# A two-layer decoder trunk: the stretch behind the experts, with tail products tile by tile, rows scaled by ScalarE, the last stores on two queues, the first gathers counted apart, and the final vector loaded in the rotary tables' place

## The reference

```python
for layer in range(2):
    # even: conv mixer + forgetting attention; odd: sparse attention, rotary on q/k and the indexer's q/k
    hp = hp + mixer(rms_norm(hp, norm_mix))          # odd: proj = h @ w_in_odd, 4*512 + 72 columns
    x2 = rms_norm(hp, norm_ffn[layer])
    # 16 experts; top group, then the top 2 experts in it; combine (m, 16) has two weights a row
    y = sum(combine[:, e:e+1] * ((silu(x2 @ w_gate[e]) * (x2 @ w_up[e])) @ w_down[e]) for e in range(16))
    hp = hp + y
y_prompt = rms_norm(hp, norm_final)                  # y * rsqrt(mean(y*y) + 1e-6) * gain
```

## Time and profile before

| | us |
|---|---|
| median of three timed runs | 1640.16 |
| lowest and highest of them | 1635.81, 1641.26 |
| the profiled execution, its own time | 1629.98 |
| span of the profile | 1628.2 |
| mean granted TensorE clock, share of full | 0.915 |

### The profile page before, as it was taken

How to read it: one execution, slowest core, us unless ns; L and a number is a source line. 1 busy time by engine, 2 the same in 40 slices (tenths; PEclk the granted TensorE clock), 3 DMA queues, 4 the chain that set the end, 5 groups by cost and what they waited for, 6 DMA issues and landing times.

```text
span 1628.2 us, 28717 instructions
## 1 busy us (share of the span) xinstructions
PE 1389.5 (85%) x11123; PEld 787.1 (48%) x11124; DVE 645.3 (40%) x1541; ACT 300.5 (18%) x773; POOL 145.7 (9%) x370
## 2 busy tenths in 40 slices
PE   7999668888958999989589987888999699998990
PEld 4444434444445554655254443455545455555650
DVE  2059944332143311111265899566412432111104
ACT  2110024332010000000111211445521000000002
POOL 0059100000000000000200000000000000000002
PEclk9999678999978999999889999799999699999995
DMA  8440127778154899999811021233332487999965
GB/s 268 173 169 1 58 67 230 226 231 297 47 201 161 326 368 368 399 398 416 309 38 52 1 100 61 76 105 105 105 155 98 141 309 286 396 386 390 404 272 197
DMA packets 86635, 341.60 MB, mean 210 GB/s; under 512 B 24791, under 2 KB 32055, under 8 KB 72534
## 3 DMA queue, kind: packets, MB, share of 16 engines
q1 hardware_dynamic: 66302, 289.80, 48.4%
q0 software_dynamic: 10656, 37.56, 6.8%
q10 hardware_dynamic: 9536, 12.33, 2.2%
HBM read 309.53 MB, written 30.47 MB: 209 GB/s over the span
## 4 chain that ended last, share of the span: by engine, by line
PE 55%; DVE 20%; DMA 10%; SPq 7%; issue 5%; ACT 2%; POOL 1%; ACTq 0%; DVEq 0%; POOLq 0%
PE banks L1098 18%; PE banks L1126 9%; PE banks L1027 7%; DVE arena L2148 6%; DMA arena<-in_wstream 6%; PE banks L796 4%; DVE arena L1665 4%; SPq L446 3%; PE banks L827 3%; DVE arena L1793 2%; SPq L472 2%; PE banks L946 2%; DMA arena<-hn_scratch,arena 2%; DVE arena L1787 1%; SPq L477 1%
## 5 line engine op out<-in xcount | busy, mean ns | idle before, releaser
L1098 PE MATMUL banks<-arena 128*32 128x128 f32 (+1 forms) x4736 | 363.3, 337 | 28.1 <-issue 17.3
L1098 PEld LDWEIGHTS banks<-arena 128*32 128x32 f32 (+1 forms) x4736 | 241.5, 127 | 148.4 <-issue 59.2
L1126 PE MATMUL banks<-arena 128*64 128x512 f32 (+1 forms) x1184 | 175.8, 503 | 1.1 <-ACT arena L1551 1.1
L1665 DVE TENSOR_TENSOR arena<-arena,banks 128x256 f32<-128x256 f32 (+5 forms) x84 | 38.9, 464 | 295.4 <-PE banks L1098 171.0
L796 PE MATMUL banks<-arena 128*128 128x512 f32 x320 | 139.9, 595 | 1.0 <-DMA arena<-in_wstream 0.9
L2042 DVE COPY arena<-banks 128x256 f32<-128x256 f32 (+1 forms) x56 | 21.4, 382 | 289.7 <-PE banks L1111 283.3
L1665 DVE TENSOR_TENSOR arena<-banks,arena 128x512 f32<-128x512 f32 (+5 forms) x159 | 70.6, 474 | 141.1 <-ACT arena L1475 86.6
L1665 DVE TENSOR_TENSOR arena<-arena 128x256 f32<-128x256 f32 (+17 forms) x248 | 98.7, 431 | 57.6 <-ACT arena L1416 36.1
L827 PE MATMUL banks<-arena 128*128 128x512 f32 x256 | 118.1, 607 | 0.0
L1027 PE MATMUL banks<-arena 128*128 128x512 f32 x256 | 111.2, 594 | 1.4 <-issue 0.8
L2148 DVE SCALAR_TENSOR_TENSOR arena<-arena 128x512 f32<-128x512 f32 x120 | 105.2, 937 | 1.1
(11 more groups left out here) (269 smaller groups left out, 1493.8 us busy)
## 6 DMA issues: line engine op xcount, KB each, us to landing
arena<-in_wstream SPq DMA_DIRECT2D x109, 2048.0 KB, 16.0
arena<-in_fox_kt SPq DMA_DIRECT2D x64, 256.0 KB, 2.9
arena<-in_fox_v SPq DMA_DIRECT2D x64, 256.0 KB, 3.0
arena<-in_dsa_page SPq DMA_DIRECT2D x64, 256.0 KB, 2.9
expert_rows<-arena ACTq DMA_DIRECT2D x76, 128.0 KB, 8.9
expert_rows<-arena POOLq DMA_DIRECT2D x1, 6656.0 KB, 20.2
hn_scratch<-arena POOLq DMA_DIRECT2D x8, 512.0 KB, 3.0
expert_rows<-arena ACTq DMA_DIRECT2D x72, 32.0 KB, 8.5
```

The lines of the kernel that those rows point to most:

```text
L1098: last = mm(bank(b, 0, 4 * n, n * j, n * j + n), x[:, c, :], w[:, c, 4 * n * j:4 * n * j + 4 * n], start=(c == 0), stop=(c == DC - 1))
L1126: last = mm(bank(3, 0, 8 * n, n * q, n * q + n), ht2[g % 2][:, 128 * i + n * j:128 * i + n * j + n], w[:, c, 8 * n * q:8 * n * q + 8 * n], ...
L1665: return v.tensor_tensor(out, x, y, op)
```

## The change

- Layer 0: TensorE's transposes and tail products alternate. It turns tile 0, then for each tile t turns tile t+1 and computes the tail products of tile t. The tail weights are waited for at the first product.
- Layer 0: the scaling of rows moves from VectorE to ScalarE (`scaled`, a copy with the inverse root as scale). VectorE only inverts the root and signals `inverse`; its loop has `NT + 2` steps and does `to_xt` for tile t-2, ahead of the reciprocal of tile t-1, for which it waits in the same step.
- SP loads tail weights and constants of layer 1 when the row numbers are known (`row_u0`) instead of when all tiles are combined. In its queue they stand behind `last_rows(0)`.
- Both layers: of the four pieces of the last part ScalarE stores two and SP the other two (`last_rows`).
- Both layers: the first gather has a semaphore of its own, `yb_first`, and VectorE waits for the first two gathers one by one.
- The final vector goes to the region of the rotary tables, the causal mask and the router weights instead of `XT`, and is issued when the normalised rows of layer 1 are stored, behind the last expert weights. It, and both tail weights, share the semaphore `c_late`.

```diff
 PER = {stem: n for n, stems in SHARED for stem in stems.split()}
-PER_PARITY = {"hn_out": (48, 32), "yb": (32,) * NT,
+PER_PARITY = {"hn_out": (48, 32), "yb": (16,) + (32,) * (NT - 1),
               "y_rows": tuple(max(STORED[i::4]) for i in range(4))}
...
     nlf = at("WORK", 4160, 64, 0, 8)
-    fin_g = at("XT", 0, 1024)
+    fin_g = at("ROPE", 0, 1024)
     yfin = [at("X", 2048 + 1024 * i, 1024) for i in range(NT)]
...
             tokens(t)
-        sp.dma_start(at("WORK", 3072, 64), a["wtail0"]).then_inc(S("c_tail0"), 16)
+        sp.dma_start(at("WORK", 3072, 64), a["wtail0"]).then_inc(S("c_late"), 16)
         sp.dma_start(bvec, a["bvec"]).then_inc(S("c_misc"), 16)
...
+        def last_rows(l):
+            s, off, n = PARTS[GROUPS - 1]
+            i, r0 = (GROUPS - 1) % 4, 32 * FIRST[s] + off
+            sp.wait_ge(S(f"y_ev{l}"), upto(f"y_ev{l}", GROUPS))
+            for q in range(64 // n, 128 // n):
+                sp.dma_start(y_d[r0:r0 + n, 8 * n * q:8 * n * q + 8 * n], y2[i][n * q:n * q + n, 0:8 * n])\
+                    .then_inc(S(f"y_rows{l}_{i}"), 16)
         def spilled(l):
...
             sp.dma_start(ring[k % RING], a["wstream"][k]).then_inc(S(f"ring{k % RING}"), 16)
+        last_rows(0)
         spilled(0)
-        sp.wait_ge(S("combined0"), NT)
-        sp.dma_start(at("WORK", 3072, 576), a["wtail1"]).then_inc(S("c_tail1"), 16)
+        sp.wait_ge(S("row_u0"), 1)
+        sp.dma_start(at("WORK", 3072, 576), a["wtail1"]).then_inc(S("c_late"), 16)
...
         experts(1)
+        sp.wait_ge(S("hn_out1_0"), upto("hn_out1_0", 48))
+        sp.dma_start(fin_g, a["fin_gain"]).then_inc(S("c_late"), 16)
+        last_rows(1)
         spilled(1)
-        sp.wait_ge(S("combined1"), upto("combined1", 1))
-        sp.dma_start(fin_g, a["fin_gain"]).then_inc(S("c_fin"), 16)
         for t, c0, c1 in TILES:
...
                                             bass.IndirectOffsetOnAxis(row_u[0:rows(t), NT * k + t:NT * k + t + 1], 0))\
-                        .then_inc(S(f"yb{l}_{t}"), 16)
+                        .then_inc(S(f"yb{l}_{t}") if i else S("yb_first"), 16)
...
                     after(job)
-            pe.wait_ge(S("c_tail0"), 16)
+            pe.wait_ge(S("c_late"), 16)
             for t, c0, c1 in TILES:
...
-            pe.wait_ge(S("c_tail1"), 16)
+            turn_h(2, 0)
             for t, c0, c1 in TILES:
+                if t + 1 < NT:
+                    turn_h(2, t + 1)
+                if t == 0:
+                    pe.wait_ge(S("c_late"), 32)
                 pe.wait_ge(S("xt2"), upto("xt2", t + 1))
...
         spilled(0)
-        for t in range(NT):
-            turn_h(2, t)
...
+            def scaled(t):
+                act.wait_ge(S("inverse"), t + 1)
+                if t - 1 > 0:
+                    act.wait_ge(S("hn_t2"), upto("hn_t2", t - 1))
+                af(hn[t % 2][0:rows(t), :], h[0:rows(t), t, :], ACT.Copy, scale=rstd[0:rows(t), t:t + 1])\
+                    .then_inc(S("hn2"), 1)
             if n == 0:
...
                         root(t - 1)
+                    if t and n == 2:
+                        scaled(t - 1)
                 else:
...
                 root(NT - 1)
+            if n == 2:
+                scaled(NT - 1)
...
                 act.wait_ge(S(f"y_ev{l}"), upto(f"y_ev{l}", g + 1))
-                for q in range(128 // n):
+                for q in range(128 // n if g < GROUPS - 1 else 64 // n):
                     act.dma_start(y_d[r0:r0 + n, 8 * n * q:8 * n * q + 8 * n], y2[i][n * q:n * q + n, 0:8 * n])\
...
             hv = h[0:rows(t), t, :]
-            dve.wait_ge(S(f"yb{l}_{t}"), upto(f"yb{l}_{t}", 32))
+            if t > 0:
+                dve.wait_ge(S(f"yb{l}_{t}"), upto(f"yb{l}_{t}", 32))
             for k in range(2):
                 i = 2 * t + k
+                if i == 0:
+                    dve.wait_ge(S("yb_first"), 16 * l + 16)
+                if i == 1:
+                    dve.wait_ge(S(f"yb{l}_0"), upto(f"yb{l}_0", 16))
                 ins = v.scalar_tensor_tensor(out=hv, in0=ybuf[i][0:rows(t), :],
...
             n = 2 * l + 2
-            for t in range(NT + 3):
+            for t in range(NT + 2):
                 if t < NT:
...
                     mean_square(n, t - 1)
-                if 2 <= t <= NT + 1 and l == 0:
-                    normed(n, t - 2)
-                if t >= 3 and l == 0:
-                    to_xt(n, t - 3)
-                if 2 <= t <= NT + 1 and l == 1:
+                if t >= 2 and l == 0:
+                    to_xt(n, t - 2)
+                if 1 <= t <= NT and l == 0:
+                    dve.wait_ge(S("root2"), upto("root2", t))
+                    cell = rstd[0:rows(t - 1), t - 1:t]
+                    v.reciprocal(cell, cell).then_inc(S("inverse"), 1)
+                if 2 <= t and l == 1:
                     final(t - 2)
...
             if t == 0:
-                dve.wait_ge(S("c_fin"), 16)
+                dve.wait_ge(S("c_late"), 48)
             v.scalar_tensor_tensor(out=yfin[t][0:rows(t), :], in0=h[0:rows(t), t, :],
```

## The result

Over 17 runs each, the kernel after has a median of 1624.83 us (1617.27 to 1629.39), the kernel before 1632.00 (1623.87 to 1646.82). The ratio is 0.9935, 95% interval [0.9913, 0.9957]: 0.65% faster, where the forecast was 0.35%. It rested on the first three runs of the kernel before, whose median of 1640.16 lies 8.2 us above that of the 17. So the time misses mainly by its starting point, and the ratio is the better measure of the change.

What follows compares the result with a forecast made beforehand. TensorE, busy 85% of the 1628.2 us span, was taken as the bound. Gains of 3.9 (layer 0) and 1.9 (layer 1) sum to 5.8 us, off a 1640.16 median: 1634.4, range 1629.5 to 1641.

Steps and rivals of the forecast that it cites:

- I take the gain as the same number of microseconds: 1634.4: Whole kernel: the 5.8 us gain is taken off the three-run median of 1640.16 us, giving 1634.4.
- so I put the rise at 823.1: Layer 0's combine: TensorE's clock returns to full at 823.1 us, 4.4 us after dense work starts.
- layer 0's 3.9: Layer 0's tail products, tile by tile: end at 834.8 against 838.7 us, 3.9 earlier; bounds 1 and 4.7.
- rival C: Layer 0: clock rises late or queue order costs more; gains 1.5 there, 1.9 in layer 1, 1636.8 us; chance 0.20.
- Rival B: Layer 0: clock stays at half, products end 4.9 us later than before; whole 1643.2 us; chance 0.08.
- Rows scaled by ScalarE: Layer 0's loop: 4.5 us a tile against 4.6, copy 1.06 us; VectorE wins nearly nothing.
- Stores: Both layers' last stores, split over two queues: 0.9 us earlier each, within 0.7 to 1.0.
- rival D: Stores gain nothing, from SP's block load or slower landing; gain 4.2 in all, 1636.0 us; chance 0.12.
- First gather apart: Both layers: VectorE's first operation comes early, but the 1.3 us is hidden by tile 1's wait; worth 0.
- constants: Layer 1's constants and tail weights, loaded before layer 0's gathers: costed at 0, or 1 us without cover.
- Final vector: Layer 1's end: early issue removes VectorE's wait, tile 3 then waits for gathers; gain 1.9 us, bounds 1.7 and 2.4.

Runs made afterwards that it cites:

- fin_late: Changed kernel with the final vector issued late, when tile 0 of layer 1 is combined: ratio 0.9934 to the kernel before.
- stores_one: Changed kernel with all four last stores on ScalarE again in both layers: ratio 0.9964 to the kernel before.
- joint_first: Changed kernel with one semaphore for both first gathers again: pieces 799.8, 44.1, 750.8, 35.0 us.
- es_late: Changed kernel with layer 1's constants loaded when all tiles are combined, tail weights still early: ratio 0.9937 to the kernel before.
- warm: Changed kernel with 24 extra matmuls, results unused, around layer 0's transposes (20, 3 and 1): ratio 0.9946 to the kernel before.
- scale_dve: Changed kernel with VectorE scaling layer 0's rows in its old loop, TensorE's new order kept: ratio 0.9952 to the kernel before.
- alternate_alone: Kernel before with only TensorE's transposes and products alternating and the tail weights loaded early: ratio 0.9963 to the kernel before.
- best3: Changed kernel with VectorE scaling rows in its old loop and layer 1's constants loaded late: ratio 0.9930 to the kernel before.
- before_again: Kernel before, no edit, profiled a second time: layer 0's piece 51.1 us.
- l0_old: Changed kernel with layer 0's loop as before (VectorE scales, all transposes, then all products): ratio 0.9949 to the kernel before.
- products_last: Changed kernel, ScalarE still scaling, but all five transposes first and then the 80 products: ratio 1.0012 to the kernel before.
- before_fill: Kernel before with 26 extra matmuls, results unused, ahead of layer 0's first three sets of transposes: ratio 0.9975 to the kernel before.
- after_again: Changed kernel, no edit, profiled and timed again: ratio 0.9914 to the kernel before.

## Why the prediction was right or wrong

**The starting point (why the time lies outside the range).** The step that failed is "I take the gain as the same number of microseconds: 1634.4". It subtracts 5.8 from 1640.16, the median of three runs; the 17 have 1632.00 and go from 1623.87 to 1646.82, so three did not fix it. From 1632.00 the same 5.8 give 1626.2, 1.4 above the measured median. The prediction had the other number too, 1624.2 from the profiled execution, and set it aside. That this one is so near is partly luck, as the terms below show.

**The clock after.** The step "so I put the rise at 823.1" failed: by the same reckoning from the eviction 28.6 us, measured 37.1, 38.1 and 37.7. The dense stretch began when forecast (24.2 us after the eviction by my numbers, 24.0 in the trace); what was wrong is that the clock rises 4.4 us behind its start. It took 13 us. Products 0 and 1 took 3.3 each and transposes 1.7. The piece is 42.5 where I had 40.3 (834.8 - 794.5); the gain in the profiled pair is 1.8, not 3.9, near rival C's 1.5. Nor is the late rise fixed. In fin_late, which has the changed kernel's layer 0, the clock rose at 28.4 us, as forecast, in the first products, and fell again at 38.6, in the last ones:

```profile
834.21 2.77 PE L829 MATMUL banks<-arena 128*128 128x72 f32 x16
```
```profile
845.36 4.88 PE L829 MATMUL banks<-arena 128*128 128x72 f32 x31
```

It fell in the last products of stores_one, joint_first, es_late and warm too. With VectorE scaling in TensorE's new order (scale_dve, alternate_alone, best3, no extra matmuls) it rose at 28.1 to 28.6 us and stayed. The rule of the Trainium skill, page "TensorE: Matmul & The Clock Gate", section "Part 1: The HAM clock gate", is that the gate follows how busy the array has been. The trace agrees only in part: the windows of before_again have PE busy 2.00 of 2.00 us from 830 on, and the clock stayed at 0.50 until the 15.9 us of products were over.

**The kernel before (missing from the prediction).** I priced it from one profile in which the 80 products ran at full clock. With all products last they stood at half clock in one of four profiles of the kernel before, and in l0_old and products_last; in before_fill the clock fell as they began. It costs 7.4 us (51.1 against a mean of 43.7). Rival B feared the half clock for the new order, when it was the old order that paid most for it: there all five sets stand behind the last rows, while in the new order three of the five lie before them. Its price for the changed kernel, 4.9 us, was not tested, since in every profile with that order the clock rose sooner than the 43.1 us after the eviction that it needs. One in four adds 1.8 us to the mean of the kernel before.

**Rows scaled by ScalarE.** Right that VectorE wins nothing: step 4.60 (4.5 forecast), copy 1.15, where the row had 1.06. The estimate of 1.13 us from the Trainium skill, page "ScalarE: Activation LUTs", section "What ACT_TABLE_LOAD costs", was the nearer. The main effect of the scaling I hadn't priced: rows come to TensorE later, and with VectorE scaling in the same order the piece is 38.6 to 39.2. The last transposes begin 35.1 us after the eviction in scale_dve, 37.1 in fin_late, where ScalarE scales and the clock rose as early, and 38.6 to 39.4 in the changed kernel. So of those 4 us about 2 are the scaling and about 2 the later rise of the clock, as an estimate from single profiles.

**Stores.** The size of the term was off: 0.9 forecast, 2.0 measured in layer 1 (5.4 to 3.4). I had held the landing at 2.97; it falls to 1.73. In layer 0 it is 1.1 in the profiled pair, where the block load landed behind the issue of SP's stores, a partial case of rival D, and 1.8 to 2.6 between the profiles of the kernel before and the two others after.

**First gather apart, constants.** 0 forecast, right in layer 1; in layer 0 worth about 1, against a loss of 1.1 to 1.8 by the constants, which I had costed at 0 with 1 as the bound.

**Final vector.** Forecast 1.9 for piece 4 as a whole; measured 3.2 in the pair, 3.7 between the means (38.1 and 34.4). What lacked is the landing of the stores and, by fin_late, that a late vector also goes with later gathers: tile 3 did not wait at all after.

**The sum.** Between the means of four profiles before and three after, layer 0's piece gives 2.7 and layer 1's 3.7, 6.4 us. Forecast: 5.8. The nearness is luck: layer 0's 3.9 is 0.8 against the three profiles of the kernel before with products at full clock, and the 1.8 that I had left out and 1.8 more in layer 1 make up for it. The medians differ by 7.2 and the ratio says 10.6 [7.0, 14.2]. The third piece gives 4.0 more (751.3 and 747.2), but no edit lies in it, and over all 20 profiles here it runs from 744.4 to 752.9, with 750.8 in one with all of the change but a semaphore. And the first piece, which has no edit either, takes 4.0 away (795.8 and 799.8). Windows of the third piece, before_again and after:

```profile
846.55:1598.00 751.45, 679.51 (x5373) 382.95 (x5369) 330.91 (x932) 158.31 (x437) 26.60 (x134) 0.94 0.50 187
```
```profile
838.82:1583.21 744.39, 672.87 (x5373) 378.11 (x5369) 330.85 (x932) 158.03 (x437) 26.50 (x134) 0.95 0.51 189
```

The same matmuls take 6.6 us less at a slightly higher mean clock. The mean granted clock that is on record for each execution says more. It is 0.9175 over the 17 of the changed kernel and 0.9176 over the 10 of after_again, but 0.9133 over the 32 of the kernel before beside the latter; a difference of 0.0042 is some 14 us more at half clock. Among the timed runs of the kernel before the slower ones have the lower clock (correlation -0.74). The four profiles of the kernel before average 0.916 and the three after 0.915, so the profiled executions lack this difference, and with it, it seems, the part of the gain that the pieces don't show. The order of the 80 products alone is not its source, for l0_old has 0.917. Whether the change has a part in it, by where in time it puts the later stages, stays open.

## What to carry to other kernels

Where TensorE begins again after a pause, a profile shows one of several outcomes of the clock; profile the kernel more than once before pricing work there, and put as little TensorE work as possible behind the last data. Take the starting point of a forecast in us from more than three runs, or forecast a ratio. Cut the execution at fixed points: pieces of 40 us show 1 us if the clock went the same way in both, where the whole varies by 10. A load whose wait is short can cost more by what it lies beside: the constants cost 1.1 to 1.8 us so.

## What the runs showed of the hardware that I had not expected

- 80 matmuls of 128x72 at 1.2 GHz kept TensorE busy for 15.9 us and the clock did not rise until they ended (before_again, l0_old, products_last). At 2.4 GHz they kept the clock in three profiles of the kernel before and lost it after 1.7 us in before_fill.
- With the same layer 0 code the clock rose 3.6 us (fin_late) or 13.1 to 13.4 us (the three profiles of the changed kernel) after TensorE's dense stretch began.
- Four 32 KB stores on one queue: the last landed 2.8 to 3.4 us after its issue, save 5.58 in stores_one; two on each of two queues: 1.70 to 1.76, save 2.70 and 2.07 in layer 0 of after and after_again, where the block load landed 2.2 and 1.6 us after the eviction.
- Code that no edit touches varied between profiles by 16 us in the first piece (791.8 to 807.6). The time at half clock in it goes from 116 to 140 us and rises with its length (correlation 0.88 over the 20 profiles). In stores_one one gather of layer 0's experts took 11.83 us there.
